# Two chained transformer blocks in float32 on one core: expert weights ordered expert by expert and begun in the second block, and the residual, gate and final norm taken into the experts' sum

## The reference, cut to what matters

```python
mix = jnp.concatenate([h_m, h_a], axis=-1) @ w_out[l]
x = x + gate1 * mix
hn2 = rms_norm(x, g_norm2[l]) * (1.0 + scale2) + shift2
ffn = hierarchical_moe(hn2, ...)   # top-1 of 4 groups, in it top-2 of 8 experts, per token:
                                   # (silu(xb @ w_gate[e]) * (xb @ w_up[e])) @ w_down[e], weighted, summed
x = x + gate2 * ffn
return rms_norm(x, g_final)
```

## Time and profile before

| | |
|---|---|
| median of 3 runs (lowest to highest) | 1094.51 us (1093.35 to 1094.53) |
| the profiled execution: its own time | 1095.95 us |
| its span, first to last instruction | 1094.2 us |
| mean granted PE clock | 0.98 |
| PE busy / DVE busy / ACT busy | 1022.7 us (93%) / 493.4 us (45%) / 389.9 us (36%) |
| transfers | 327.87 MB, 300 GB/s over the span |

### The profile page before, as it was taken

How to read it: one execution, slowest core, us unless ns; L and a number is a source line. 1 busy time by engine, 2 the same in 40 slices (tenths; PEclk the granted TensorE clock), 3 DMA queues, 4 the chain that set the end, 5 groups by cost and what they waited for, 6 DMA issues and landing times.

```text
span 1094.2 us, 13601 instructions
## 1 busy us (share of the span) xinstructions
PE 1022.7 (93%) x5616; PEld 700.9 (64%) x5616; DVE 493.4 (45%) x683; ACT 389.9 (36%) x575; POOL 22.3 (2%) x42
## 2 busy tenths in 40 slices
PE   5999999999999999798999699999999999999883
PEld 4888878888999888697787444444444444443331
DVE  4477667987967745765645511111111111101003
ACT  5644544446435443664734221111111111111112
POOL 0000000010000000100000000000000000000000
PEclk9999999999999999898999799999999999999997
DMA  9977448976887655354444699999999999999991
GB/s 332 338 256 258 160 164 294 315 268 224 287 300 260 235 198 187 104 179 127 181 154 162 265 405 421 421 421 421 422 420 421 421 420 422 421 420 421 422 394 45
DMA packets 86305, 327.87 MB, mean 300 GB/s; under 512 B 5744, under 2 KB 5776, under 8 KB 61536
## 3 DMA queue, kind: packets, MB, share of 16 engines
q1 hardware_dynamic: 84896, 323.45, 77.0%
q0 software_dynamic: 1344, 3.50, 1.0%
HBM read 325.88 MB, written 1.05 MB: 299 GB/s over the span
## 4 chain that ended last, share of the span: by engine, by line
PE 40%; DMA 13%; DVE 3%; ACT 2%; issue 1%; DVEq 0%; ACTq 0%
PE bank L899 15%; DMA e_wlo<-in_w_expert_up 8%; PE bank L922 7%; PE bank L868 3%; DMA es<-in_w_expert_up 3%; DMA raw<-in_w_expert_up 2%; PE bank L937 2%; PE bank L539 2%; PE bank L540 2%; PE bank L543 1%; PE bank L908 1%; PE bank L511 1%; PE bank L515 1%; PE bank L514 1%; PE bank L883 1%
## 5 line engine op out<-in xcount | busy, mean ns | idle before, releaser
L1441 DVE TENSOR_TENSOR wlo<-raw,whi 128x2048 fp32r<-128x2048 f32 x90 | 205.9, 2290 | 105.8 <-ACT whi L985 105.2
L985 ACT ACTIVATE whi<-raw 128x2048 fp32r<-128x2048 f32 x90 | 171.6, 1912 | 98.3 <-PE bank L515 37.9
L2032 DVE SCALAR_TENSOR_TENSOR YL<-bank,wsl,YH 128x512 fp32r<-128x512 f32 x32 | 24.0, 751 | 269.1 <-ACT YH L1369 269.1
L899 PE MATMUL bank<-raw,XT 128*64 128x512 f32 x400 | 90.8, 596 | 5.2 <-DMA raw<-in_w_expert_up 5.2
L899 PE MATMUL bank<-e_whi,XT 128*64 128x512 f32 x192 | 88.5, 604 | 6.7 <-DMA e_wlo<-in_w_expert_up 6.7
L514 PE MATMUL bank<-wlo,hh 128*128 128x512 f32 x224 | 88.5, 395 | 2.9 <-DVE wlo L1441 2.9
L511 PE MATMUL bank<-whi,hh 128*128 128x512 f32 x224 | 89.2, 398 | 1.0 <-ACT whi L985 1.0
L899 PE MATMUL bank<-e_wlo,XT 128*64 128x512 f32 x192 | 88.6, 605 | 0.0
L515 PE MATMUL bank<-whi,hl 128*128 128x512 f32 x224 | 88.3, 394 | 0.0
L539 PE MATMUL bank<-fh,whi 128*128 128x256 f32 x256 | 73.6, 287 | 1.2 <-DVE fl L1611 1.2
L1430 DVE SCALAR_TENSOR_TENSOR ada_acc<-raw,silu_c,ada_acc 128x512 f32<-128x512 f32 x96 | 72.0, 750 | 2.5
(11 more groups left out here) (359 smaller groups left out, 1902.5 us busy)
## 6 DMA issues: line engine op xcount, KB each, us to landing
raw<-in_w_in SPq DMA_DIRECT2D x42, 1024.0 KB, 5.4
raw<-in_w_ff SPq DMA_DIRECT2D x32, 1024.0 KB, 5.4
raw<-in_w_expert_gate SPq DMA_DIRECT2D x25, 1024.0 KB, 22.3
raw<-in_w_expert_up SPq DMA_DIRECT2D x25, 1024.0 KB, 23.0
raw<-in_w_ada SPq DMA_DIRECT2D x24, 1024.0 KB, 5.9
e_whi<-in_w_expert_gate SPq DMA_DIRECT2D x24, 1024.0 KB, 24.2
e_wlo<-in_w_expert_up SPq DMA_DIRECT2D x24, 1024.0 KB, 25.2
raw<-in_w_expert_down SPq DMA_DIRECT2D x22, 1024.0 KB, 25.2
```

Of the source, the lines that this page charges most:

```text
L899: m = e.matmul(b[64 * w:64 * w + 64, :], K.XT[j // 4 % 2][:, k, j % 4, :], K.weights(halves[w])[:, 512 * c:512 * c + 512], start=k == 0, s ...
L985: e.activation(whi[n % RING][:, :], raw[h.raw][:, :], ACT.Copy).then_inc(S["hi"], 1)
L1441: e.tensor_tensor(wlo[n % RING][:, :], raw[h.raw][:, :], whi[n % RING][:, :].bitcast(F32), ALU.subtract).then_inc(S["lo"], 1)
```

## The change: what it does

- **Raw buffers.** From half 96 (`LATE`) on, halves use raw buffers 0 to 2 in turn, and each waits for the half that was in its buffer before (three back). Raw 3, 4, 5 become buffers of the experts.
- **Early loads.** Behind halves 98, 99, 100 and 101 SP issues the experts' loads 0, 1, 2, 3 (to es12, raw 3, 4, 5), and behind half 112 load 4 (to es7). The other 187 follow after half 113. There are still 16 buffers, in another order.
- **Order.** The loads of an expert stand together: gate and up (first halves), gate and up (second halves), down, down. PE's order of use isn't changed. `used_up` gives the count of `eused` at which each load has been used.
- **Sum.** Four matmuls by the identity, `keep_x`, put x into the `moe` banks ahead of the experts, two before the matmuls of the rank and two behind them. Combine adds to that. `gate2q` holds gate2 with columns 0 to 511 on partitions 0 to 63 and the others on 64 to 127, as down's result lies. DVE now first writes `YS` = down's result x weight x gate2q, ACT copies it to `YH`, and DVE writes `YL = YS - YH`.
- **End.** No drain, no `ysc`, no addition. Combine signals after its first two banks (`comb_t0`) and after the others (`comb`). ACT squares the banks, DVE writes `fin` from the banks. The overflow count is read one step earlier, and the memset ahead of the last square root stands before the experts.

```diff
+LATE = 96
 class Half:
-        self.raw = i % RAW
-        self.loaded = 16 * (i // RAW + 1)
+        self.raw, self.before = raw, before
+        self.loaded = before.loaded + 16 if before else 16
...
+            raw = i % RAW if i < LATE else i % (RAW // 2)
+            half = Half(i, kind, src, chunks, info, len(self.of[kind]), raw, self.in_raw.get(raw))
...
         for base, n, one in ((0, NE, fixed), (NE, NOV, moving)):
+            for j in range(n):
+                for w, hf in ((0, 0), (1, 0), (0, 1), (1, 1), (2, 0), (2, 1)):
+                    one(j, w, hf)
             for j in range(n + 1):
-                for hf in range(2 if j < n else 0):
-                    one(j, 0, hf)
-                    one(j, 1, hf)
+                for w, hf in ((0, 0), (1, 0), (0, 1), (1, 1)) * (j < n):
+                    n_used += 1
+                    self.used_up[base + j, w, hf] = n_used
                 for hf in range(2 if j > 0 else 0):
-                    one(j - 1, 2, hf)
+                    n_used += 1
+                    self.used_up[base + j - 1, 2, hf] = n_used
...
         buffer(slot("es12", 12, [128, 2048]), "es12", 0)
-        buffer(slot("es7", 7, [128, 2048]), "es7", 0, "mix_mm", MIX["m"] + 4)
-        for h in self.halves[-RAW:]:
-            buffer(self.raw[h.raw], f"raw{h.raw}", h.loaded, "lo", h.nth + 1)
+        for r in (*range(RAW // 2, RAW), None, *range(RAW // 2)):
+            if r is None:
+                buffer(slot("es7", 7, [128, 2048]), "es7", 0, "mix_mm", MIX["m"] + 4)
+            else:
+                h = self.in_raw[r]
+                buffer(self.raw[r], f"raw{r}", h.loaded, "lo", h.nth + 1)
...
+    def keep_x(t, q):
+        free(f"moe{2 * t + q}")
+        e.wait_ge(S["x"], X_AT["3"] + 2 * t + q + 1)
+        e.matmul(K.at[f"moe{2 * t + q}"][0][:, :], C("ident"), K.x[:, t, 512 * q:512 * q + 512], start=True, stop=False,
+                 skip_group_check=True)
+    keep_x(0, 0)
+    keep_x(0, 1)
...
     e.matmul(b[:, 32:64], C("ones"), MK[:, 0, :], start=False, stop=True, skip_group_check=True).then_inc(S["route_mm"], 1)
+    keep_x(1, 0)
+    keep_x(1, 1)
...
-            m.then_inc(S["comb"], 1)
+                m.then_inc(S["comb" if t else "comb_t0"], 1)
...
-    e.drain().then_inc(S["all_done"], 1)
...
 act_program:
         def down(j):
-            e.wait_ge(S["eused"], K.half_of[j, 2, 1] + 1)
-            e.wait_ge(S["pt"], 2 * j + 2)
+            e.wait_ge(S["ys"], j + 1)
             if j:
                 e.wait_ge(S["comb"], j)
-            e.activation(K.YH[:, :], K.at[f"down{j}"][0][:, :], ACT.Copy,
-                         scale=K.wsl[:, j % 4:j % 4 + 1]).then_inc(S["yh"], 1)
+            e.activation(K.YH[:, :], K.YS[:, :], ACT.Copy).then_inc(S["yh"], 1)
...
 dve_program:
         def down(j):
+            e.wait_ge(S["eused"], K.used_up[j, 2, 1])
+            e.wait_ge(S["pt"], 2 * j + 2)
+            e.scalar_tensor_tensor(out=K.YS[:, :], in0=K.at[f"down{j}"][0][:, :], scalar=K.wsl[:, j % 4:j % 4 + 1],
+                                   in1=K.gate2q[:, :], op0=ALU.mult, op1=ALU.mult).then_inc(S["ys"], 1)
             e.wait_ge(S["yh"], j + 1)
-            e.scalar_tensor_tensor(out=K.YL[:, :], in0=K.at[f"down{j}"][0][:, :], scalar=K.wsl[:, j % 4:j % 4 + 1],
-                                   in1=K.YH[:, :].bitcast(F32), op0=ALU.mult, op1=ALU.subtract).then_inc(S["yl"], 1)
+            e.tensor_tensor(K.YL[:, :], K.YS[:, :], K.YH[:, :].bitcast(F32), ALU.subtract).then_inc(S["yl"], 1)
...
 act_program, behind the experts:
     for t in range(2):
+        e.wait_ge(S["comb" if t else "comb_t0"], NE)
         for n in range(2):
-            e.wait_ge(S["x"], X_AT["4"] + 2 * t + n + 1)
-            squares(K.x[:, t, 512 * n:512 * n + 512], 8 * t + n, K.fin[:, t, 512 * n:512 * n + 512])
-    for t in range(2):
+            e.activation(K.sqx[:, t, 512 * n:512 * n + 512], K.at[f"moe{2 * t + n}"][0][:, :], ACT.Square,
+                         scale=1.0 / 32, accum_out=stat(8 * t + n)).then_inc(S["sq"], 1)
         root(10 + t, 8 * t, 1)
...
 dve_program, behind the experts:
+        e.scalar_tensor_tensor(out=stat(k), in0=stat(k), scalar=EPS, in1=stat(k + 1), op0=ALU.add,
+                               op1=ALU.add).then_inc(S["ms"], 1)
+        e.wait_ge(S["sd"], 10 + t)
+        e.reciprocal(stat(k), stat(k)).then_inc(S["rs"], 1)
...
-            e.scalar_tensor_tensor(out=K.fin[:, t, o], in0=K.x[:, t, o], scalar=stat(k), in1=K.gfb[:, o], op0=ALU.mult,
-                                   op1=ALU.mult).then_inc(S["fin"], 1)
+            e.scalar_tensor_tensor(out=K.fin[:, t, o], in0=K.at[f"moe{2 * t + n}"][0][:, :], scalar=stat(k),
+                                   in1=K.gfb[:, o], op0=ALU.mult, op1=ALU.mult).then_inc(S["fin"], 1)
...
 sp_program:
+        o = h.before
+        if o:
...
-            e.wait_ge(S["eused"], i - n + 1)
+            e.wait_ge(S["eused"], K.used_up[K.experts[i - n][1:]])
...
+    early = {LATE + 2 + k: k for k in range(4)}
+    early[len(K.halves) - 2] = 4
     for h in K.halves:
         load(h)
-    for i in range(K.n_static):
+        if h.i in early:
+            load_expert(early[h.i], K.experts[early[h.i]][0])
+    for i in range(len(early), K.n_static):
         load_expert(i, K.experts[i][0])
```

More of the change, by code:

```diff
@@ L60, with __init__ @@
 class Half:
[L63 removed]
+    def __init__(self, i, kind, src, chunks, info, nth, raw, before):
         self.i, self.kind, self.src, self.chunks, self.info = i, kind, src, chunks, info
         self.nth = nth
[L66 to L67 removed]
+        self.raw, self.before = raw, before
+        self.loaded = before.loaded + 16 if before else 16
 class Sems(dict):
@@ L219, in order_weights @@
         A, self.halves, self.of, n_ada = self.A, [], {"mm": [], "ada": []}, [0]
-        self.half_of = {}
+        self.half_of, self.in_raw = {}, {}
         def add(kind, src, chunks, info=None):
-            self.of[kind].append(Half(len(self.halves), kind, src, chunks, info, len(self.of[kind])))
-            self.halves.append(self.of[kind][-1])
+            i = len(self.halves)
+            raw = i % RAW if i < LATE else i % (RAW // 2)
+            half = Half(i, kind, src, chunks, info, len(self.of[kind]), raw, self.in_raw.get(raw))
+            self.in_raw[raw] = half
+            self.of[kind].append(half)
+            self.halves.append(half)
         def cols(w, r0, c0):
@@ L271, in expert @@
             self.half_of[j, w, hf] = len(self.experts)
-            self.experts.append((src, j))
+            self.experts.append((src, j, w, hf))
         def fixed(e, w, hf):
@@ L442, in place_psum @@
         use("x3T11", (6, "h2T_d", 1))
-        use("rank", (7, "rt", 22))
-        use("moe", *[(4 + k, "moe_out", k + 1) for k in range(4)])
+        use("rank", (0, "rt", 22))
+        for k in range(4):
+            use(f"moe{k}", (4 + k, "fin", k + 1))
         def block_uses(base, n):
@@ L462, in block_uses @@
                 if j > base:
-                    use(f"down{j - 1}", (3, "yl", j))
+                    use(f"down{j - 1}", (3, "ys", j))
         block_uses(0, NE)
@@ L936, in combine @@
                         r = slice(64 * q, 64 * q + 64)
-                        m = e.matmul(K.at["moe"][2 * t + q][:, :], K.PT[j % 4][r, 128 * t:128 * t + 128], y[r, :],
-                                     start=j == 0 and y is K.YH, stop=j == base + n - 1 and y is K.YL,
-                                     skip_group_check=True)
-            m.then_inc(S["comb"], 1)
+                        m = e.matmul(K.at[f"moe{2 * t + q}"][0][:, :], K.PT[j % 4][r, 128 * t:128 * t + 128], y[r, :],
+                                     start=False, stop=j == base + n - 1 and y is K.YL, skip_group_check=True)
+                m.then_inc(S["comb" if t else "comb_t0"], 1)
         for q in range(4):
@@ L1385, in blocks @@
         gathered(base // 4, 3)
+        count = None
         for j in range(base, base + n + 2):
+            if j == NE:
+                e.wait_ge(S["ovf"], 1)
+                count = e.value_load(K.ovf[0:1, 0:1], min_val=0, max_val=NOV - 1)
             if base + 1 < j:
@@ L1395, in blocks @@
                 gate_up(j)
-    blocks(0, NE)
-    e.wait_ge(S["ovf"], 1)
-    count = e.value_load(K.ovf[0:1, 0:1], min_val=0, max_val=NOV - 1)
+        return count
+    count = blocks(0, NE)
     with e.If(count > 0):
         blocks(NE, NOV)
+        e.wait_ge(S["comb"], NE + NOV)
     e.wait_ge(S["warm"], 1)
@@ L2040, in blocks @@
         one_hots(base // 4 + 1)
+        count = None
         for j in range(base, base + n + 2):
+            if j == NE:
+                e.wait_ge(S["ovf"], 2)
+                count = e.value_load(K.ovf[0:1, 0:1], min_val=0, max_val=NOV - 1)
             if base + 1 < j:
@@ L2051, in blocks @@
                 one_hots(j // 4 + 2)
-    blocks(0, NE, RK)
-    e.wait_ge(S["ovf"], 2)
-    count = e.value_load(K.ovf[0:1, 0:1], min_val=0, max_val=NOV - 1)
+        return count
```

(5 more changed lines are left out.)

47 lines of the change are left out of this document (22 added, 25 removed).

## The result

Measured: 1099.59 us median (1099.13 to 1103.51, 6 runs), against 1094.52 for the kernel before in the same comparison. The ratio is 1.0061, 95% interval 1.0047 to 1.0076. So the change costs 5.1 us by the medians and 6.7 by the ratio (0.61% of 1094.5), where 2.9 were forecast. The profiled execution took 1099.6 us, its span 1097.8.

A forecast was written before the change was run, and what follows sets the result against it. The stream of expert weights was taken to bound the kernel. Terms 4.9 + 5.0 - 0.4 + 0.7 + 0.75 - 7.4 - 0.7 = +2.9 us took the median from 1094.51 to 1097.4 us (0.27% slower), range 1093.8 to 1100.3.

The forecast's parts named there:

- What bounds the kernel: Experts' stage: the stream of expert weights sets its end, and the moment the stream becomes continuous (load 16) sets the stream.
- The early loads: Loads 0 to 4 issued earlier: nothing waits for them, and block two is not starved by three raw buffers; 0.
- a hole at the start: Load 20 waits for down's buffer of expert 0, so the stream stops after load 19; +4.9 us (4.2 to 5.8).
- Two loads later at the end: The up half that `gate_up(31, 0)` needs becomes load 187 instead of 185; +5.0 us.
- x put into the banks: Four `keep_x` around the rank, before the first expert: PE's start moves between -1.4 and +1.4 us; -0.4 taken.
- The split of down's result: Longer split, unhidden twice at the end: +0.7 us before combine(30), +0.75 up to the last YH.
- The end: From the last YH's end to the span's end: 10.1 us instead of 17.5; -7.4 us.
- The last wait: `gate_up(31, 0)` ran slow (5.11 us, not 3.65) after PE's last transfer wait; half of 1.5 us gained, -0.7.
- The hole realigns: Rival: the hole lets lagging transfer engines catch up, so all 6.5 us of lateness could go; 1090.9 us, chance 0.08.
- Half clock under `keep_x`: Rival, before the first expert: `keep_x` delays the gather by 1.4 us and the hole is 5.8; 1100.1 us, chance 0.09.
- the order costs nothing: Rival, experts' stage: PE does not wait for the stream, so the 4.9 and 5.0 fall away; 1087.5 us, chance 0.03.
- The "same" case: Rival, whole kernel: within 0.2%, with hole 4.2, start -1.4 and no slow matmuls after the last wait; 1094.9 us, chance 0.27.

The follow-up runs named there:

- the tail alone: Kernel before with only the loads of down(30) moved ahead of gate and up of expert 31; 1101.22 us, ratio 1.0058.
- end_only: Changed kernel, new sum and end kept, with the loads as before the change (old order, no early loads, six raw buffers); 1090.22 us, ratio 0.9966.

## Why the prediction was right or wrong, point by point

**What bounds the kernel: right.** What the order takes from the stream arrives at `gate_up(31, 0)`: 6.65 us by the windows of 20 us, 6.6 by its start.

**The early loads, 0: not contradicted in the profile, open in the medians.** Load 7 is issued at 589.97 (589.86 before); PE doesn't start sooner beyond the scatter (619.60, 620.35, 619.32, 616.97, 619.28 with them, 619.87, 619.05, 620.43 without, all with the new end; 0.7 us between the means, nearly all of it from the 616.97). In all comparisons the versions with them are the faster, by 1.2 to 2.5 us (the 1.2 and 1.6 across two comparisons), where 0 was forecast; the cause stays open. Block two isn't starved, that much is shown.

**The order, a hole at the start, 4.9: the first step that failed, by size.** Where, when and why were right: no issue between 629.0 and 639.6, next to no data from 636 on. But it measures 6.6 (445.27 against 438.71) between two kernels that are otherwise alike, and 5.8 to 6.7 over all pairs: at or above the upper bound of 5.8. By the windows from 620 to 660 the changed kernel moved 11.7 MB, with the three windows behind them (424, 424 and 421 GB/s) 14.2: at 421 GB/s 6.1 us. The step took the stream to be full from 641.5 on. What it was is read best from two kernels that differ in nothing else near the hole. Windows of 2.5 us of the new order alone:

```profile
635.00:637.50 2.50, 2.50 (x16) 0.79 (x12) 0.00 (x0) 0.50 (x2) 0.00 (x0) 1.00 0.18 72
637.50:640.00 2.50, 2.50 (x14) 0.79 (x12) 0.00 (x0) 0.60 (x1) 0.00 (x0) 1.00 0.00 0
640.00:642.50 2.50, 2.50 (x14) 0.86 (x12) 0.27 (x1) 0.69 (x1) 0.00 (x0) 1.00 0.61 187
642.50:645.00 2.50, 2.50 (x14) 0.75 (x10) 0.48 (x1) 0.00 (x0) 0.00 (x0) 1.00 1.06 318
...
657.50:660.00 2.50, 2.50 (x14) 0.92 (x11) 0.26 (x2) 0.00 (x0) 0.00 (x0) 1.00 0.97 390
```

and of the new order from expert 8 on:

```profile
635.00:637.50 2.50, 2.50 (x14) 0.83 (x12) 0.00 (x0) 0.46 (x2) 0.00 (x0) 1.00 1.03 426
637.50:640.00 2.50, 2.50 (x16) 0.79 (x14) 0.00 (x0) 0.60 (x1) 0.00 (x0) 1.00 0.99 419
640.00:642.50 2.50, 2.50 (x14) 0.83 (x12) 0.31 (x1) 0.69 (x1) 0.00 (x0) 1.00 0.97 383
642.50:645.00 2.50, 2.50 (x14) 0.79 (x10) 0.44 (x1) 0.00 (x0) 0.00 (x0) 1.00 0.99 413
...
657.50:660.00 2.50, 2.50 (x15) 0.95 (x12) 0.23 (x2) 0.00 (x0) 0.00 (x0) 1.00 1.02 426
```

The difference of each pair, times 2.5 us, over 421 GB/s: 2.10, 2.49, 1.16, 0.56 and 0.21, 6.5 us in all (the windows left out in between add 0.1). The first three are the hole (5.75, near the upper bound); the others are a restart below the full rate and a second thin place. For the thin place SP's timeline of the changed kernel suggests the cause: the next release comes at 654.29, 14.7 us after 639.59, and the six loads between cover 14.9, so "no second hole" held by next to nothing. For the restart too: load 21 comes 1.7 us after 20, as PE uses the two down halves one after the other, and up to then one load is alone under way. Neither was tried by itself. And the choice of 4.9 out of 4.2 to 5.8 gave the new stream credit for stalls that the old one had (360 GB/s at 640 to 645 in the earlier trace rows); the kernel above has 383 and 413 there. So the hole was paid with more than its own length.

**Two loads later at the end, 5.0: right, within the scatter** (4.9 between the two kernels that are alike, 4.2 on the mean of all; 1059.75 - 620.84 = 438.9 in the tail alone as well).

**x put into the banks, -0.4: right in size, and by luck in this pair of profiles.** The first expert starts at 619.60 against 619.97, but the matmuls of the rank had already begun 0.76 us sooner (610.79, L883, against 611.55). From there to the first expert this pair shows 8.81 us against 8.42, which is a loss. The earlier trace rows was the short case: the five other profiles without `keep_x` have 9.48 to 9.58 there. Of the eight with it seven have 8.75 to 9.22, and one 7.01. The means are 8.67 and 9.35, so some 0.7 us are won. The half-clock end of the range, +1.4, came in none of them, though in the seven the second pair of `keep_x` ran at half, as here: the gather then begins 0.6 us later after the rank, but comes up to its full rate sooner (from 616.40, in the earlier trace rows from 617.69). The full-clock end came once, in the repeated version with early loads in order of use: 7.01, 1.4 below. Windows of 2 us, PE alone, of the changed kernel show the clock's fall from its upper level (2.4 GHz) to its lower one:

```profile
608.00:610.00 2.00, 0.00 (x0) 0.86 1.00 408
610.00:612.00 2.00, 1.21 (x5) 0.50 1.03 403
```

The fall came while PE stood idle. The Trainium skill (TensorE: Matmul & The Clock Gate, "What's actually happening") has the clock set by how busy PE has been recently; that agrees. But the four added matmuls had it up before the gather in one profile of eight only.

**The split of down's result, +1.45: right for the engines' own times, but what comes behind it was put at nothing, the second step that failed.** From `gate_up(31, 0)` to the last YH's end: 20.1 in the second profile of the kernel before, 21.5 in the first one with the order of use (1052.88 to 1074.39). But in six of the seven profiles that have the new split and keep PE's order, `down(31)` took 4.47 to 5.30 us; in all others, where PE waits 1.1 us or less ahead of the step, some 3.65. The longer split makes PE wait 1.75 us (end_only's timeline), and then the granted clock falls:

```profile
1069.18 0.50 PE L967 MATMUL bank<-YH,PT 64*128 64x512 f32 x2 [1.75 <-DVE YL L2072]
```

Windows of 2 us, PE alone, of the changed kernel:

```profile
1078.00:1080.00 2.00, 0.41 (x4) 1.00 0.00 0
1080.00:1082.00 2.00, 2.00 (x12) 0.62 0.00 0
1082.00:1084.00 2.00, 2.00 (x6) 0.52 0.00 0
```

In the three profiles of versions with the new order and end `down(31)` took 4.71 to 5.11 us, 1.3 more than 3.61 on the mean. So the split costs some 2.8 us at the end, not 1.45. Taking the wait away took the slow matmuls away, in one profile. That the wait makes them slow is thereby borne out, not proven: one profile has the wait and no slow matmuls.

**The end, -7.4: right** (-7.2). Inside it two small errors cancel: the last fin ends 7.0 us after YH instead of 7.6, and from there to the end of the span are 3.3 us instead of 2.5.

**The last wait, -0.7: wrong, the third step that failed.** The 5.11 us of the earlier trace rows were an accident of that execution (3.65 in the second profile; slow in four of fourteen profiles of all versions, two of seven in order of use and one of four with the new order throughout). The forecast counted half of it as a gain, while a like amount arises in `down(31)`.

**The sum.** With what was measured, as means over the profiles: hole 6.3, tail 4.2, `keep_x` -0.7, split 1.45, slow `down(31)` 1.3, end -7.2, last wait 0: +5.4. The medians say 5.1 and the ratio 6.7. Of the 2.5 us above the forecast's 2.9 the hole makes 1.4, `down(31)` 1.3 and the last wait 0.7; the tail and `keep_x`, a little better than forecast, take 1.1 back (the end is 0.2 short of its -7.4).

Against the one execution that the prediction rests on it is only +3.6, 0.7 from the forecast, and that closeness is luck: that execution was 1.4 us above its kernel's median, by its late last load and its slow `gate_up(31, 0)`, while the profiled one of the changed kernel is its median. The forecast took the same 1.4 off the changed kernel's time. `gate_up(31, 0)` at 1064.31 lay in the forecast's 1063 to 1066 because the undersized hole and the late load of the earlier trace rows cancelled there.

**The rivals.** The hole realigns nothing: it costs more than its own length. Half clock under `keep_x` came, in seven profiles of eight, without its price. That the order costs nothing is refuted. The "same" case needed a short hole; it was longer.

## What to carry to other kernels

A queue that issues in order waits with all that stands behind its head. An order of loads that puts the next issue behind a buffer which is released late opens a hole, and where the transfers are what the kernel waits for, each byte not moved there is paid at the end, with the restart: here some 6.3 us, none if the same order begins in mid-stream. Load in the order in which buffers are released, and put what the last compute step needs as early in that order as it can be.
Before a sum is built on one execution, its last steps are worth comparing with a second one: two executions of the kernel before lay 3 us apart, as much as the whole forecast.

## What was not expected of the hardware

In six of seven profiles a wait of PE of 1.75 us, with little work around it, was followed by a `down(31)` at a lower granted clock (5.11 us instead of 3.65 in the changed kernel); waits of 1.1 and 0.98 us in its place never were. The length of a wait doesn't settle it alone: ahead of the last combine PE waited 2.34 us in the changed kernel, and that combine's matmuls ran at the full rate (0.44 us a pair, 0.42 before). The same kernel went both ways in two executions (3.61 and 4.47 us). The Trainium skill, same page and section, says that the point at which the clock changes varies from run to run; that agrees.

When the stream came back after the hole, the DMA engines showed a full share (1.06) for 2.5 us while only 318 GB/s moved (new order alone, 642.5 to 645), where the full stream has 421 at a share of 1.01. Why is open.
